# Two moves in GpSimd's queue of a two-layer decoder trunk: where heads 2 and 5 are staged

## The chip, the core and the metric

One core of a Trainium2 chip runs the whole program. The time is the device time of one execution in microseconds (us); lower is better. Engines are named as the profile names them: PE is TensorE (PEld its weight loads), DVE is VectorE, ACT is ScalarE, POOL is GpSimd, SP is SyncE, which issues transfers. Each engine works through its own queue in order and meets the others at semaphores only.

## What is computed

Two layers (`DEPTH = 2`) over one sequence of 512 rows of width 1024, all in float32. Cut to what matters here:

```
for l in range(2):
    h    = rms_norm(x) * (1 + sc) + sh
    proj = h @ w_in[l]
    y_ssd  = Mamba-2 scan: 4 chunks of 128 rows, 8 heads of 64, SiLU gate, grouped RMS norm
    y_mla  = 4 heads, q and k of width 96 from low-rank (latent) projections with rotary part,
             RMS norm of q and k per head, dense causal attention
    y_moba = 4 heads, q and k of width 64 straight from proj, RMS norm per head,
             causal attention with a bias by distance
    x = x + g * (concat(norm(y_ssd), norm(y_mla), norm(y_moba)) @ w_out[l])
    x = x + g' * mixture_of_experts(...)      # 16 experts, top 2
```

## The kernel before, in words

A hardware loop runs the same program for both layers. In a layer the stages follow one another: the input projection, the mixers (this case), the output projection, the router and the experts. The mixer stage is written as one order by hand for each engine.

**Heads.** The eight attention heads are taken in the order `HEADS = [6, 7, 4, 5, 0, 1, 2, 3]`: the number h that the code passes around (0 to 7) is the place in this list. Places 0 to 3 are the four MoBA heads, places 4 to 7 the four MLA heads. "The third head" is h = 2, a MoBA head; "the sixth" is h = 5, the second MLA head. For each head:

- `stage(h)` on GpSimd (from L2417) multiplies the head's rows of q and k by their reciprocal norms and writes them to a pair of row buffers, `staged(h)`: two instructions for a MoBA head (both recorded at L2415), three for an MLA head. MoBA heads use `moba_rows[h % 2]` in slot 2 of `ring`, MLA heads use `mla_rows[h % 2]` in `work`. For h in 2, 3, 6, 7 it first waits until the head two places before it has been turned (`qk_ps`). It ends by counting up `stg`.
- `turn_q(h)` and `turn_k(h)` on TensorE (L1042, L1054) wait for `stg` and transpose the rows; VectorE (`q_out`, L2030) and ScalarE (`k_out`, L1515) take them out.
- `scores(n)` on TensorE (L1069), n = 4 h + t for the row tiles t = 0 to 3; `biased(n)` on VectorE (L2045) adds the bias and takes the maximum; `expo(n)` on ScalarE (L1527); `turn_p(n)` (L1084) and `pv(n)` (L1100) on TensorE; `head_out(h)` on VectorE (L2050, L2051).

**Chunks.** The first four heads run beside the four chunks c = 0 to 3 of the scan, head c beside chunk c. A chunk has `xs_rows` (L960), `decay` (L975, L978), `bm_rows` (L966, L968), `y_off` (L986), `state` (L998) and `y_diag` (L1012) on TensorE, and `chunk_dt` (L1947, L1949), `decay_difference` (L1957), `chunk_scores` (L1967), `chunk_y` (L1986, L1987) and others on VectorE. `turn_q(c + 1)` stands right behind `y_off(c)` in TensorE's queue. `y_diag(c)` counts up `yd_ps`; `chunk_y(c)` counts up `y_dn`. The buffers of a chunk are doubled (`xs`, `xdt`, `xde`, index c % 2): `xs` is `work[s0 : s0 + 1024]`, `xdt` is `work[s0 + 1024 : s0 + 2048]`. `skip(c)` (L2409) on GpSimd makes the product of `xs` with the skip weights for chunk c.

**Latent projections.** Beside chunk 0 TensorE makes the MLA q and k/v rows (`mla_qkv(0)` to `(3)`, L1028, L1031), ScalarE copies them out and counts up `qkv_ev` to 8 (L1505, L1507). Then GpSimd turns the rotary parts (`rope(0)` to `rope(4)`, six instructions each, L2449 to L2456, done: `kr_dn`), VectorE sums the squares (`mla_squares`, L2007 and L1923, done: `hss`), and GpSimd takes the power -1/2 (`rstd`, L2369, L2370).

**Late modulation.** Between its other work VectorE adds up the modulation of the next half (`late_adds`, L1735, L1739, three additions to two tiles), from chunk 2 on.

**Behind the chunks** come the tiles n = 16 to 31 of the MLA heads. For n = 16 TensorE's queue begins with `turn_q(5)`, `turn_k(5)`, `scores(18)`, `turn_p(16)`, `pv(15)`.

**GpSimd's queue** in this stage, before (each `wait` blocks all that stands behind it):

```
stage(0)  store_ada_rows(1)  skip(0)  stage(1)
wait qkv_ev 8   rope(0) rope(1) skip(1) rope(2) rope(3) rope(4)
stage(2)  skip(2)   wait hss 2   rstd   stage(3)  skip(3)  stage(4)
wait y_dn 4   stage(5)   wait ysq 8   rstd   y_norm ...  stage(6)  y_norm ...  stage(7)
```

Of the kernel before, what the change touches and what calls it, by code (L numbers as in the profile page):

```python
# [112 lines left out]
def trunk(nc, A, out, cpack, bucket_oh, relv, hf_rows, y_rows, mod_rows):  # L113
# [10 lines left out]
    def sem(name):  # L124
        sems.append(ctx.enter_context(nc.semaphore(name)))
        return sems[-1]
# [28 lines left out]
    def view(off, *dims, of=work):  # L155
        n = int(np.prod(dims))
        v = of[:, off:off + n]
        if len(dims) == 2:
            return v.rearrange("p (a b) -> p a b", a=dims[0])
        if len(dims) == 3:  # L160
            return v.rearrange("p (a b c) -> p a b c", a=dims[0], b=dims[1])
        return v
# [5 lines left out]
    s0 = 10944  # L168
# [13 lines left out]
    p_cols = [actT[:, 6:8, :], view(16384, 2, 512)]  # L182
    y_scratch = view(s0 + 768, 256)
    moba_rows = [[ring[:, 2, 2816 + 512 * n + 256 * m:3072 + 512 * n + 256 * m] for m in range(2)] for n in range(2)]
    mla_rows = [[view(18624 + 384 * m, 384) for m in range(2)], [view(s0 + 384 * m, 384) for m in range(2)]]
    rtmp = ring[:, 2, 0:1280].rearrange("p (a b) -> p a b", a=4)
    sq = ring[:, 2, 1280:2816]
    sq_moba = view(17408, 1024)
# [60 lines left out]
    def hi_chunk(j, k):  # L249

        _, a0, _, buf = next(h for h in hi_parts if h[0] == j and h[1] <= k < h[2])
        return buf[:, 512 * (k - a0):512 * (k - a0) + 512]
# [122 lines left out]
    yd_ps = sem("y_diag_in_psum")  # L375
# [298 lines left out]
    def staged(h):  # L674
        q, k = moba_rows[h % 2] if h < 4 else mla_rows[h % 2]
        return tuple(a.rearrange("p (t n) -> p t n", t=T) for a in (q, k))
# [15 lines left out]
    with nc.Fori(0, DEPTH) as L:  # L692
# [3 lines left out]
        with nc.Block() as block:  # L696
# [154 lines left out]
            def _(pe):  # L851
# [55 lines left out]
                for i, b in enumerate(IN_ORDER):  # L907
                    wd = in_width[b]
                    w_parts = [in_part(b, half) for half in range(2)]
                    for t in range(T):  # L910
                        n = group_no[("in", b, t)]
                        bank_free(n)
                        if i == 0:
                            pe.wait_ge(hl_dn, 2 * t + 2)
                        for k in range(KD):
                            if i and t == 0 and k % 4 == 0:
                                pe.wait_ge(in_w_lo, 2 * i + k // 4 - 1)
                            if i == 0 and k == 4 and t < T - 1:
                                to_columns(t + 1)
                            _, lo, hi = (ap.rearrange("p (k n) -> p k n", k=4)[:, k % 4, :] for ap in w_parts[k // 4])  # L920
                            hh, hl = actT_r[:, k, :], hL[:, k, :]
                            for m, (w_, h_) in enumerate(((hi, hl), (lo, hh), (hi, hh))):
                                first_, last_ = k == 0 and m == 0, k == KD - 1 and m == 2
                                if b in (1, 2):
                                    mm = pe.matmul(ps[n % 2][:, :], w_[:, P * t:P * t + P], h_, start=first_, stop=last_)
                                else:
                                    mm = pe.matmul(ps[n % 2][:, 0:wd], h_[:, P * t:P * t + P], w_, start=first_, stop=last_)  # L927
                        mm.then_inc(acc_ps, 1)
                        if n == T:
                            pe.wait_ge(hl_dn, 2 * T)  # L930
                            pe.wait_ge(par, 14 * 16)
                            pe.transpose(ps[2][:, 0:64], prow[:], cst[0:64, C_ID:C_ID + 64]).then_inc(pcol_ps, 1)
                        if n in ADA_AFTER:
                            ada_total(ADA_AFTER[n], ps[6 + ADA_AFTER[n] % 2])
# [255 lines left out]
                def out_products(b, t, ks, opens=False, closes=False):  # L1190
                    n = group_no[("out", b, t)]
                    for k in ks:
                        if t == 0 and k % 4 in (0, 2):
                            pe.wait_ge(out_w_lo, 2 * b + k // 4 + 1)
                        _, lo, hi = (ap.rearrange("p (k n) -> p k n", k=4)[:, k % 4, :] for ap in out_part(b, k // 4))
                        yh, yl = (ap[:, k, P * t:P * t + P] for ap in (actT_r, yL))
                        pe.matmul(ps[n % 2][:, :], yl, hi, start=opens and k == ks[0], stop=False)
                        pe.matmul(ps[n % 2][:, :], yh, lo, start=False, stop=False)
                        mm = pe.matmul(ps[n % 2][:, :], yh, hi, start=False, stop=closes and k == ks[-1])
                    if closes:  # L1200
                        mm.then_inc(acc_ps, 1)
# [1162 lines left out]
            def _(g):  # L2364
# [37 lines left out]
                def skip(c):  # L2402
                    g.wait_ge(xs_cp, c + 1)
                    if c > 0:
                        g.wait_ge(y_dn, c)
                    else:
                        g.wait_ge(h_ps, 2 * T)
                        g.wait_ge(par, 14 * 16)
                    g.tensor_tensor(xd.rearrange("p (h n) -> p h n", h=NH), xs[:, c % 2, :].rearrange("p (h n) -> p h n", h=NH),  # L2409
                                    hpar[:, 2, :].unsqueeze(2).to_broadcast([P, NH, HP]), ALU.mult).then_inc(xd_dn, 1)  # L2410
# [3 lines left out]
                def times_rstd(dst, src, rstd_, n):  # L2414
                    return g.tensor_tensor(dst, src, rstd_.to_broadcast([P, T, n]), ALU.mult)  # L2415

                def stage(h):  # L2417

                    if h in (2, 3, 6, 7):
                        g.wait_ge(qk_ps, 2 * h - 2)  # L2420
                    q3, k3 = staged(h)
                    hd = HEADS[h]
                    hh = hd % MH
                    c0 = 0 if hd < MH else 32
                    rq = rs_h[:, c0:c0 + 16].rearrange("p (t h) -> p t h", t=T)[:, :, hh:hh + 1]
                    rk_ = rs_h[:, c0 + 16:c0 + 32].rearrange("p (t h) -> p t h", t=T)[:, :, hh:hh + 1]
                    if hd < MH:
                        if hd == 0:
                            g.wait_ge(hrs, 2)
                        step(times_rstd(q3, qrow[:, :, DQ * hh:DQ * hh + DQ], rq, DQ))  # L2430
                        step(times_rstd(k3[:, :, 0:DN], kv[:, :, 128 * hh:128 * hh + DN], rk_, DN))
                        times_rstd(k3[:, :, DN:DQ], kr, rk_, DR).then_inc(stg, 1)
                    else:
                        step(times_rstd(q3[:, :, 0:HP], proj[:, :, MQ0 + HP * hh:MQ0 + HP * hh + HP], rq, HP))
                        times_rstd(k3[:, :, 0:HP], proj[:, :, MK0 + HP * hh:MK0 + HP * hh + HP], rk_, HP).then_inc(stg, 1)
                    g.wait_ge(stg, h + 1)
# [8 lines left out]
                def rope(h):  # L2445
                    src = qrow[:, :, DQ * h + DN:DQ * h + DQ] if h < MH else proj[:, :, KR0:KR0 + DR]
                    x1, x2 = src[:, :, 0:16], src[:, :, 16:32]
                    ta, tb, tc, td = (rtmp[:, k, 64 * h:64 * h + 64].rearrange("p (t n) -> p t n", t=T) for k in range(4))
                    g.tensor_tensor(ta, x1, cos, ALU.mult).then_inc(gch, 1)  # L2449
                    g.tensor_tensor(tb, x2, sin, ALU.mult).then_inc(gch, 1)  # L2450
                    g.tensor_tensor(tc, x1, sin, ALU.mult).then_inc(gch, 1)
                    g.tensor_tensor(td, x2, cos, ALU.mult).then_inc(gch, 1)
                    step.n += 4
                    g.wait_ge(gch, step.n)
                    step(g.tensor_tensor(x1, ta, tb, ALU.subtract))
                    ins = g.tensor_tensor(x2, tc, td, ALU.add)  # L2456
                    if h < MH:
                        step(ins)
                    else:
                        ins.then_inc(kr_dn, 1)  # L2460
# [4 lines left out]
                store_ada_rows(1)  # L2465
                skip(0)
                stage(1)
                g.wait_ge(qkv_ev, 2 * T)
                rope(0)
                rope(1)  # L2470
# [1 line left out]
                rope(2)  # L2472
                rope(3)
                rope(4)
                stage(2)
                skip(2)
                g.wait_ge(hss, 2)
                rstd(rs_h[:, 0:32], ss_h[:, 0:32], DQ, hrs)
                stage(3)
                skip(3)  # L2480
                stage(4)
                g.wait_ge(y_dn, T)
                stage(5)
                g.wait_ge(ysq, 8)
                rstd(rs_y[:, 0:8], ss_y[:, 0:8], 256, yrs)
                g.wait_ge(yrs, 1)
# [110 lines left out]
```

## Time and profile before

| what | value |
|---|---|
| median of 3 runs | 1477.59 us (1475.14 to 1477.91) |
| span of the profiled execution | 1470.7 us |
| PE busy | 1323.4 us, 90% |
| DVE busy | 1162.9 us, 79% |
| ACT busy | 739.2 us, 50% |
| POOL busy | 239.1 us, 16% |
| DMA | 382.29 MB, mean 260 GB/s |
| mixer stage, layer 0 | about 190 to 333 us of the span |
| mixer stage, layer 1 | about 901 to 1040 us of the span |

The span is from the first to the last instruction of one execution. A row of the timeline gives the start, the time busy, the engine, the line, the operation and its operands, how many instructions were merged, and in brackets how long the engine stood idle before it and who released it. A releaser is inferred from semaphore events.

### The profile page before, as it was taken

To read this page: it belongs to the slowest core of one execution; us is meant where nothing else is said; L and a number is where in the kernel's file an instruction comes from. 1 tells how busy PE (TensorE), PEld (TensorE's weight loads), DVE (VectorE), ACT (ScalarE), POOL (GpSimd) and SP (SyncE) were. 2 spreads that over 40 slices of the span, in tenths; PEclk is the share of its full clock that TensorE was granted. 3 is DMA by queue.
4 is the path that set the end of the run, shared out by engine and by line. 5 is a ranking of instruction groups with operands and counts; after the bars stand their busy time and mean duration, and the time that the engine had idled before them with its cause. 6 is when DMAs were issued, how large, how long until landed. Compare 5 with 4: busy or idle time off the path is not lost. (4 is left out here: it accounts for less than half of the span.)

```text
span 1470.7 us, 17413 instructions
## 1 busy us (share of the span) xinstructions
PE 1323.4 (90%) x6467; PEld 1048.2 (71%) x6467; DVE 1162.9 (79%) x1379; ACT 739.2 (50%) x969; POOL 239.1 (16%) x296
## 2 busy tenths in 40 slices
PE   6799987889989999999949998878998999999993
PEld 2577865667878888888747777566777788888871
DVE  3569856885579999999855988488656999999986
ACT  1334333562437777777413343447223877777750
POOL 0100125431011000000121012345110100000002
PEclk9899988989999999999979999898999999999996
DMA  9676621433579999999558483133347999999965
GB/s 357 240 261 223 203 90 59 143 100 131 218 283 361 413 411 416 407 402 376 196 180 294 170 270 120 58 115 115 130 152 287 362 404 407 413 404 407 403 225 197
DMA packets 96788, 382.29 MB, mean 260 GB/s; under 512 B 6009, under 2 KB 8807, under 8 KB 86968
## 3 DMA queue, kind: packets, MB, share of 16 engines
q1 hardware_dynamic: 73144, 311.50, 55.9%
q0 software_dynamic: 15232, 55.63, 9.7%
q10 hardware_dynamic: 8320, 13.96, 2.7%
q8 instruction: 55, 0.90, 0.2%
q14 instruction: 37, 0.30, 0.1%
HBM read 348.25 MB, written 32.82 MB: 259 GB/s over the span
## 5 line engine op out<-in xcount | busy, mean ns | idle before, releaser
L1274 PE MATMUL ps<-mod_rounded,work_rounded 128*128 128x512 f32 x340 | 136.9, 403 | 1.1 <-DVE work_rounded L2281 1.1
L1276 PE MATMUL ps<-mod_rounded,work_rounded 128*128 128x512 f32 x340 | 134.4, 395 | 0.0
L1275 PE MATMUL ps<-ring_rounded,work_rounded 128*128 128x512 f32 x288 | 113.7, 395 | 0.0
L1735 DVE SCALAR_TENSOR_TENSOR gain<-ring,csil,gain 128x512 f32<-128x512 f32 x134 | 104.3, 778 | 3.3
L2140 DVE TENSOR_TENSOR ring_rounded<-ring,mod_rounded 128x2048 fp32r<-128x2048 f32 (+1 forms) x54 | 102.8, 1929 | 1.4
L1275 PE MATMUL ps<-work_rounded 128*128 128x512 f32 x256 | 101.0, 395 | 0.0
L2140 DVE TENSOR_TENSOR work_rounded<-work,mod_rounded 128x2048 fp32r<-128x2048 f32 (+1 forms) x48 | 91.3, 1930 | 9.6 <-ACT mod_rounded L1635 8.4
L927 PE MATMUL ps<-ring_rounded,actT_rounded 128*128 128x512 f32 (+1 forms) x256 | 93.4, 365 | 0.0
L2512 POOL DMA_INDIRECT work<-ffn_rows,slot_idx x34 | 42.0, 1234 | 302.9 <-PE ps L1260 270.1
L1635 ACT ACTIVATE mod_rounded<-ring 128x2048 fp32r<-128x2048 f32 (+1 forms) x54 | 85.9, 1625 | 0.0
L1276 PE MATMUL ps<-actT_rounded,work_rounded 128*128 128x512 f32 x204 | 80.4, 394 | 0.0
L1655 ACT ACTIVATE work_rounded<-ps 128x512 fp32r<-128x512 f32 x68 | 37.2, 596 | 85.7 <-PE ps L1260 85.7
L927 PE MATMUL ps<-work_rounded,mod_rounded 128*128 128x512 f32 (+1 forms) x192 | 76.6, 399 | 4.0 <-ACT work L1402 4.0
L1274 PE MATMUL ps<-actT_rounded,work_rounded 128*128 128x512 f32 x204 | 80.1, 393 | 0.0
L1635 ACT ACTIVATE mod_rounded<-work 128x2048 fp32r<-128x2048 f32 (+1 forms) x48 | 76.4, 1624 | 0.0
L1274 PEld LDWEIGHTS ps<-mod_rounded,work_rounded 128*128 128x128 f32 x340 | 64.0, 188 | 15.1 <-DVE work_rounded L2281 1.6
L1276 PEld LDWEIGHTS ps<-mod_rounded,work_rounded 128*128 128x128 f32 x340 | 63.9, 188 | 14.7
L901 PE MATMUL ps<-cst 128*128 128x128 f32 x360 | 51.2, 303 | 24.2 <-issue 14.6
L927 PE MATMUL ps<-work_rounded,actT_rounded 128*128 128x512 f32 (+1 forms) x192 | 72.5, 377 | 0.0
L2140 DVE TENSOR_TENSOR ring_rounded<-ring,actT_rounded 128x3072 fp32r<-128x3072 f32 x18 | 60.4, 3356 | 12.2 <-ACT actT_rounded L1635 12.2
L901 PEld LDWEIGHTS ps<-cst 128*128 128x128 f32 x360 | 48.1, 216 | 26.8 <-issue 26.7
L2527 POOL DMA_DIRECT2D expert_rows<-work x32 | 18.1, 566 | 298.3 <-DVE work L2275 298.3
(370 smaller groups left out, 3635.9 us busy)
## 6 DMA issues: line engine op xcount, KB each, us to landing
ring<-in_ada_w SPq DMA_DIRECT2D x38, 1024.0 KB, 5.2
ring<-in_moe_w_gate SPq DMA_DIRECT2D x18, 2048.0 KB, 10.1
ring<-in_moe_w_up SPq DMA_DIRECT2D x18, 2048.0 KB, 10.4
ring<-in_moe_w_down SPq DMA_DIRECT2D x18, 2048.0 KB
work<-in_moe_w_up SPq DMA_DIRECT2D x16, 2048.0 KB, 10.6
work<-in_moe_w_down SPq DMA_DIRECT2D x16, 2048.0 KB, 11.6
work<-in_moe_w_gate SPq DMA_DIRECT2D x16, 2048.0 KB, 10.3
expert_rows<-work POOLq DMA_DIRECT2D x32, 512.0 KB, 7.7
```

Source lines behind the costliest of these rows:

```text
L901: pe.matmul(ps[7][:, 0:P], ident, ident, start=True, stop=True)
L927: mm = pe.matmul(ps[n % 2][:, 0:wd], h_[:, P * t:P * t + P], w_, start=first_, stop=last_)
L1274: pe.matmul(ps[j][:, :], xl, hi, start=k == 0, stop=False)
L1275: pe.matmul(ps[j][:, :], xh, lo, start=False, stop=False)
L1276: mm = pe.matmul(ps[j][:, :], xh, hi, start=False, stop=k == KD - 1)
L1635: a.activation(buf, slots[3 * odd + j][:, 512 * k0:512 * k1], ACT.Copy).then_inc(w_hi, 1)
L1655: a.activation(xeT_r[:, 4 * j:4 * j + 4, :], ps[2 + j][:, :].rearrange("p (k n) -> p k n", k=4), ACT.Copy).then_inc(xt_ev, 1)
L1735: add(v.scalar_tensor_tensor(acc, w, csil[:, k:k + 1], acc, ALU.mult, ALU.add))
L2140: v.tensor_tensor(slots_r[3 * odd + j][:, 512 * k0:512 * k1], slots[3 * odd + j][:, 512 * k0:512 * k1], buf.bitcast(F32), ALU.subtract).th ...
L2512: g.indirect_dma_start(out=dst, out_offset=None, in_=hf_rows, in_offset=bass.IndirectOffsetOnAxis(ap=col, axis=0)).then_inc(sem_, 16)
L2527: g.dma_start(yv[e - 4], ysb[:, e % 2, :]).then_inc(yw[e % 2], 16)
```

## The change

Three edits. `stage(2)` moves in GpSimd's queue from behind `rope(4)` to directly behind `stage(1)`, which is ahead of the wait for `qkv_ev`. `stage(5)` moves from behind the wait `y_dn >= 4` to ahead of it, and gets a wait of its own, `yd_ps >= 3`. And the second row buffer pair of the MLA heads, used by h = 5 and 7, moves its k rows from `work[s0 + 384 : s0 + 768]` to `work[s0 + 1024 : s0 + 1408]`: before, they lay across both `xs` buffers, of which the second belongs to chunk 3; after, q lies on `xs[0]` and k on `xdt[0]`, which belong to chunk 2, the third.

```diff
-    mla_rows = [[view(18624 + 384 * m, 384) for m in range(2)], [view(s0 + 384 * m, 384) for m in range(2)]]
+    mla_rows = [[view(18624 + 384 * m, 384) for m in range(2)], [view(s0 + 1024 * m, 384) for m in range(2)]]
...
                 skip(0)
                 stage(1)
+                stage(2)
                 g.wait_ge(qkv_ev, 2 * T)
...
                 rope(4)
-                stage(2)
                 skip(2)
...
                 stage(4)
+                g.wait_ge(yd_ps, 3)
+                stage(5)
                 g.wait_ge(y_dn, T)
-                stage(5)
                 g.wait_ge(ysq, 8)
```

## Rows read from the trace of the kernel before

**Rows 1.** The page: span, and busy time of an engine, share, instructions

```profile
span 1470.7 us, 17413 instructions
...
PE 1323.4 (90%) x6467; PEld 1048.2 (71%) x6467; DVE 1162.9 (79%) x1379; ACT 739.2 (50%) x969; POOL 239.1 (16%) x296
```

**Rows 2.** Waits of PE, 186 to 349: us in total, times, longest

```profile
PE ps L1042 <- POOL ring L2415: 5.2, 1, 5.2
...
PE ps L1042 <- POOL work L2415: 2.7, 1, 2.7
```

**Rows 3.** Timeline of GpSimd, layer 0

```profile
197.08 1.66 POOL L2415 TENSOR_TENSOR ring<-work,sml 128x256 f32<-128x256 f32 x2
...
222.88 1.30 POOL L2449 TENSOR_TENSOR ring<-actT,cst 128x64 f32<-128x64 f32 x1 [24.14 <-ACT mod L1507]
...
236.20 1.32 POOL L2415 TENSOR_TENSOR ring<-work,sml 128x256 f32<-128x256 f32 x2
...
257.72 1.67 POOL L2415 TENSOR_TENSOR ring<-work,sml 128x256 f32<-128x256 f32 x2
...
271.88 0.91 POOL L2415 TENSOR_TENSOR work<-work,sml 128x128 f32<-128x128 f32 x1
283.15 1.21 POOL L2415 TENSOR_TENSOR work<-actT,sml 128x384 f32<-128x384 f32 x1 [10.37 <-DVE work L1987]
...
285.47 0.41 POOL L2415 TENSOR_TENSOR work<-work,sml 128x128 f32<-128x128 f32 x1
```

**Rows 4.** Timeline of PE, layer 0, and the last row from layer 1

```profile
197.74 0.63 PE L1054 MATMUL ps<-cst,ring 128*64 128x128 f32 x4 [1.78 <-DVE mod L2030]
...
231.26 1.08 PE L986 MATMUL ps<-work 128*128 128x256 f32 x4
237.57 1.06 PE L1042 MATMUL ps<-cst,ring 128*64 128x128 f32 x4 [5.23 <-POOL ring L2415]
...
263.51 1.90 PE L1012 MATMUL ps<-work 128*128 128x64 f32 x16
...
282.35 0.87 PE L1069 MATMUL ps<-mod 96*128 96x128 f32 x4
285.93 0.64 PE L1042 MATMUL ps<-cst,work 128*96 128x128 f32 x4 [2.70 <-POOL work L2415]
...
944.14 1.06 PE L1042 MATMUL ps<-cst,ring 128*64 128x128 f32 x4 [5.24 <-POOL ring L2415]
```

**Rows 5.** Stretches: length, busy us (x) by engine, granted clock, DMA share, GB/s

```profile
199.67:231.26 31.59, 28.72 (x126) 17.76 (x126) 12.12 (x28) 13.10 (x34) 7.91 (x17) 0.84 0.30 102
910.64:937.82 27.18, 24.32 (x126) 16.00 (x126) 12.10 (x28) 13.14 (x34) 7.91 (x17) 1.00 0.37 127
231.26:246.96 15.70, 10.47 (x54) 7.63 (x53) 5.47 (x10) 2.86 (x7) 5.55 (x17) 0.67 0.00 1
...
258.87:266.30 7.43, 7.43 (x53) 6.11 (x53) 6.63 (x14) 2.97 (x7) 0.51 (x1) 1.00 0.12 31
...
291.81:298.43 6.62, 6.62 (x23) 5.12 (x24) 5.52 (x8) 5.29 (x18) 6.19 (x6) 0.51 0.25 66
```

**Rows 6.** Timeline of VectorE, layer 0

```profile
247.50 1.75 DVE L1923 TENSOR_TENSOR ring<-actT 128x1536 f32<-128x1536 f32 x1
...
284.95 0.29 DVE L2045 CUSTOM_DVE_ANT_0 mod<-ps,cst 128x128 f32<-128x128 f32 x1
...
286.61 0.75 DVE L2030 TENSOR_SCALAR mod<-ps,pcol 96x512 f32<-96x512 f32 x1 [1.36 <-PE ps L1042]
...
299.07 0.75 DVE L2030 TENSOR_SCALAR mod<-ps,pcol 96x512 f32<-96x512 f32 x1 [1.64 <-PE ps L1042]
```

**Rows 7.** L1967 (190 to 285), L1735 (282 to 284.9): min/median/max ns, starts

```profile
L1967 DVE TENSOR_TENSOR work<-work x8: 672/681/1073, 198.2 to 278.2; 128x512 f32<-128x512 f32 x8
...
L1735 DVE SCALAR_TENSOR_TENSOR gain<-ring,csil,gain x2: 744/974/1205, 282.9 to 283.7; 128x512 f32<-128x512 f32 x2
```

## The prediction

> **What bounds the kernel now.** I read the page first. The span is 1470.7 us and TensorE is busy for 90% of it, GpSimd for 16% [rows 1]. So a change that only moves GpSimd's work can gain just where TensorE stands still for GpSimd, and the question is how much it stands, where, and what is late next. The waits of TensorE in one mixer stage answer the first part: it waits for the staging line twice, 5.2 us once (MoBA rows, `ring`) and 2.7 us once (MLA rows, `work`) [rows 2]. The timeline of TensorE puts them: 5.23 us ahead of `turn_q(2)` at 237.57, and 2.70 us ahead of `turn_q(5)` at 285.93; layer 1 repeats the first with 5.24 us at 944.14 [rows 4]. GpSimd's timeline shows the other side: it idles 24.14 us until 222.88, when the latent projections have been copied out, then does the ropes up to 236.20, and `stage(2)` stands behind them and takes 1.32 us; later it idles 10.37 us until 283.15 and then does `stage(5)`, which ends at 285.47 + 0.41 = 285.88 [rows 3]. TensorE starts 0.05 us after that. Both waits are on the path: before 237.57 and before 285.93 VectorE and ScalarE have nothing left either that TensorE's next result doesn't release.
>
> Third, the windows, for the clock. The stretch from `y_off(1)` to the next chunk's first scores, 231.26 to 246.96, takes 15.70 us at a mean granted clock of 0.67; the same sequence one chunk later, 258.87 to 266.30, takes 7.43 us at 1.00 [rows 5]. So the 5.23 us are not all: the wait is followed by work at TensorE's lower level of 1.2 GHz instead of 2.4 (four transposes in 1.06 us at 237.57, against 0.63 at 197.74 [rows 4]).
>
> **Edit A, `stage(2)` ahead of the latent wait.** It removes two instructions from behind the ropes and adds them behind `stage(1)`. Its own wait, that `turn_k(0)` has been done, ends at 197.74 + 0.63 = 198.37 [rows 4]; `stage(1)` ends at 197.08 + 1.66 = 198.74 [rows 3]. So `stage(2)` runs from 198.74 to about 200.1 and GpSimd is back at its wait 22 us before that ends: the ropes, `skip(1)` and the rest are not delayed. Nothing else is in the queue that it passes (no transfer is issued between the two places).
> - Gain: `turn_q(2)` follows `y_off(1)` directly, as `turn_q(3)` follows `y_off(2)`. Chunk 1 then looks like chunk 2: 15.70 - 7.43 = **8.27 us**, of which 5.23 is the wait and 3.04 the work at the lower clock. The chunk that I compare with has even more VectorE work in it (x14 against x10 [rows 5]), so it is no flattering model.
> - What is late next? `mla_squares(1)` on VectorE needs the ropes. It starts at 247.50 [rows 6] and would start at 239.2; the ropes end at 236.20. The cover is 3.0 us. The ropes still to be done at 232 now run beside VectorE work instead of beside nothing; if they stretch by more than 3 us, the surplus is lost. After that `stage(3)` waits for these squares, so it moves with them: it ends at 257.72 + 1.67 = 259.39 [rows 3], and `turn_q(3)` comes behind `y_off(2)`, which starts at 258.87 and needs about 1 us; the margin of half a us is kept because both sides hang on the same `chunk_y(1)`.
> - Cost: the new place is busy on VectorE. `chunk_scores(0)` has two instructions of L1967. The median of the eight in the four chunks is 0.68, the longest takes 1.07 [rows 7]; asked for alone it is the first, at 198.2, beside `stage(1)` [rows 3]. The second, up to 199.9, will run beside `stage(2)` and `y_diag(0)` waits for it. I take the row's own stretch, 1.07 - 0.68 = 0.39 us; the bounds are 0 and 2 x 0.39. A gain is excluded: nothing there waits for GpSimd.
>
> The Trainium skill's page "SBUF - State Buffer", section "Who interferes with whom", speaks against this edit: VectorE with two SBUF inputs and GpSimd take a shared port pair in turn, and the later one blocks for the whole instruction of the other. By that rule L1967 would wait for what is left of the first instruction of `stage(2)`, some 0.2 us as an estimate, and edit A would stand 0.2 us better. In the row here GpSimd's side stretched too (1.66 us for `stage(1)` against 1.32 for `stage(2)`), so the trace does not fit a lock with one loser, and the rows decide.
>
> Edit A: 8.27 - 0.39 = **7.88 us a layer**.
>
> **Edit B, `stage(5)` ahead of `y_dn`, on other buffers.** The buffer edit costs nothing in itself: same shapes, same instructions. The new wait, `yd_ps >= 3`, is met when `y_diag(2)` is done, 263.51 + 1.90 = 265.41 [rows 4], while `stage(4)` ends at 271.88 + 0.91 = 272.79 [rows 3]. So it costs nothing, and nothing queued behind it (the `y_dn` wait, `rstd`, the eight `y_norm`s, `stage(6)`) is held: all of it waited beyond 283 before. `stage(5)` runs from 272.8 to about 275.5.
> - Gain: TensorE's 2.70 us are not given back whole, since VectorE is next. TensorE is done with its scores at 282.35 + 0.87 = 283.22 [rows 4] and turns q of head 5 by 283.9. VectorE must first finish two late additions and `biased(16)` at 284.95 [rows 6]. The additions take 744 and 1205 ns, the second beside `stage(5)` [rows 7]; without it they take 2 x 0.74, so `biased(16)` starts 0.46 earlier, at 284.49, and ends at 284.78. Then `q_out(5)` follows at once, where it stood at 286.61 [rows 6]: 286.61 - 284.78 = **1.83 us**.
> - Cost: in its new place `stage(5)` meets `chunk_scores(3, 0)`, L1967 again, at 272.9, and the following `decay_difference` carries a stretch on to ScalarE and TensorE. 0 to 0.46 us (the stretches seen); I take 0.39.
>
> Edit B: 1.83 - 0.39 = **1.44 us a layer**. If the first additions of n = 16 are not relieved it is 1.0, and 2.7 is the most that the wait holds.
>
> **Sum.** 7.88 + 1.44 = 9.32 us a layer, 18.6 for two. The loads of the mixer and of the experts are issued on counts that move with the work, and those issued at a fixed time are used over 20 us later, so I expect no stage behind to give any of it back. The profiled execution has 1470.7 us of span; 1470.7 - 18.6 = 1452.1. The median of the runs lies 1477.6 - 1470.7 = 6.9 us above the span. That gives **1459.0 us**, -1.26%.
>
> **Rivals.**
> 1. *The clock falls once or twice more, or once in another place.* The chain of chunk 0 shows the price: 31.59 us at 0.84 in layer 0 and 27.18 at 1.00 in layer 1, for the same instructions [rows 5], 4.41 us. Everything in layer 1 will sit about 10 us earlier, and the fall of layer 0 may appear there too: 1463.4; with a second one 1467.8. The Trainium skill, page "TensorE: Matmul & The Clock Gate", section "What's actually happening", says that the point at which the clock rises varies between runs of the same kernel. By that the falls may land anew after any shift. The trace agrees so far as the two layers differ in chunk 0. Against it: the later stretches cost the same in both layers.
> 2. *The clock gives back more.* From 291.81 to 298.43 TensorE works at 0.51, and VectorE idles 1.64 us for it at 299.07 [rows 5, 6]. If the fuller stretch around 284 keeps the clock up, that wait goes in both layers: 3.3 us more, 1455.7; with the cost terms at their lower bounds 1454.1, and if layer 0's fall in chunk 0 went too (nothing ahead of it changes), about 1450.
> 3. *Only the wait goes.* The clock stays at the lower level through chunk 1: 5.23 instead of 8.27, 6.1 us less in all, 1465.1. Rows against it: the clock fell only in the gap itself (the stretches before have 0.84 and 1.00, and TensorE was packed up to 231).
> 4. *The wait moves.* `turn_q(2)` or what follows finds something equally late, so the change doesn't do what it says: 1475 to 1478. For it: the queue is dense with waits. Against it: `q_sb`, `k_sb` and `stg` are all that `turn_q(2)` asks for, and the first two are met before 221.
> 5. *Slower.* One mechanism: with the packing changed, TensorE drops to its lower level in the chunks and stays there. Each such fall costs 4.41 us; it decides from the fifth on (18.6 / 4.41 = 4.2), which gives 1481 and more. The stage has three of them a layer now. Port stretches can't do it alone: ten VectorE instructions at 0.46 each are 4.6 us a layer, half the gain.
>
> **How the numbers follow.** Forecast 0.47 (its own range, from the bounds of the costs and one small shift of the clock, 1455.5 to 1462.5), rival 1 0.23, rival 2 0.17, rival 3 0.06, rival 4 0.04, rival 5 0.03. Taking in rivals 1 and 3 up to two falls and rival 2 but for its far end, the range is 1451 to 1468. It leaves out some 0.12. A measurement of this kernel tells about 0.2% (3 us) from no change. All cases but 4 and 5 lie below 1474.6: faster 0.93, the same 0.04, slower 0.03.
>
> **What would show it.** Right for A: `turn_q(2)` starts within 0.2 us of the end of `y_off(1)`, no wait of TensorE on the `ring` rows, the stretch from `y_off(1)` to the next chunk's scores takes 7.4 to 8 us at a clock near 1.00, and L2415 appears at 198.7. Right for B: `stage(5)` at 272.8 less the shift, no wait on it, `q_out(5)` right behind `biased(16)`. Wrong: `y_diag(0)` later by over 0.8 us, the ropes ending after `chunk_y(1)`, or the mixer stage of layer 1 not being shorter by about the same as that of layer 0. If the stretches outside the mixer stages change their lengths by over a us, my claim that nothing behind gives anything back is wrong.

## The result

The changed kernel took 1467.4 us in the median of five runs (1457.55 to 1468.42), against 1477.59; the ratio is 0.9932, 95% interval 0.9908 to 0.9956. Run again beside the experiments it took 1461.5 (six runs, 1452.01 to 1470.34; ratio 0.9892, 0.9863 to 0.9922). The kernel before took 1475.7 us in the mean of the 57 runs made beside the experiments (1475.8 with the five made beside the first result) and the changed one 1462.9 in the mean of all its 11. The change is worth **12.8 us, 0.9%**. The forecast was 18.6 us. The sign held, and so did the range (1451 to 1468), but by 0.6 us for the first median of 1467.4, which is luck; the size did not.

The profiled execution of the changed kernel is its fastest of the first five: a span of 1455.9 us, 1457.55 with what lies around it. That is 1.65 us around the span, so 5 of the 6.9 us that the prediction set between the span and the median of the kernel before were no overhead: its profiled execution was a fast one too. (Over its 57 runs the time lies 1.6 to 2.9 us above the span.)

Of the page of the changed kernel, against [rows 1]:

```profile
span 1455.9 us, 17415 instructions
...
PE 1319.3 (91%) x6467; PEld 1045.3 (72%) x6467; DVE 1162.8 (80%) x1379; ACT 738.9 (51%) x969; POOL 246.8 (17%) x296
```

GpSimd does the same 296 instructions, but is busy 7.7 us longer: some of them now run beside VectorE and stretch.

The waits of TensorE in layer 0, 186 to 349 (us in total, times, longest), against [rows 2]:

```profile
PE ps L1084 <- ACT mod L1527: 6.8, 8, 2.1
PE ps L1069 <- DVE sml L2045: 6.5, 7, 1.8
PE ps L1165 <- DVE work_rounded L2105: 1.9, 2, 1.3
```

Both waits for the staging line L2415, 7.9 us, are gone. The waits for L1527 and L2045 grew by 2.1 us together (5.4 to 6.8 and 5.8 to 6.5); no single new wait took the place of the two. The timelines of GpSimd and of TensorE, against [rows 3, 4]:

```profile
200.29 3.99 POOL L2415 TENSOR_TENSOR ring<-work,sml 128x256 f32<-128x256 f32 x4
221.70 1.30 POOL L2449 TENSOR_TENSOR ring<-actT,cst 128x64 f32<-128x64 f32 x1 [17.42 <-ACT mod L1507]
...
236.72 0.32 POOL L2456 TENSOR_TENSOR work<-ring 128x64 f32<-128x64 f32 x1
...
266.14 0.83 POOL L2415 TENSOR_TENSOR work<-actT,sml 128x384 f32<-128x384 f32 x1
```

```profile
230.07 1.08 PE L986 MATMUL ps<-work 128*128 128x256 f32 x4
230.99 0.60 PE L1042 MATMUL ps<-cst,ring 128*64 128x128 f32 x4
...
250.19 1.06 PE L1042 MATMUL ps<-cst,ring 128*64 128x128 f32 x4
```

`stage(2)` is the second half of the row at 200.29 and GpSimd is back at the latent wait 17 us ahead of its end; `stage(5)` begins at 266.14 directly behind `stage(4)`. `turn_q(2)` starts at 230.99, in the tail of `y_off(1)`, in 0.60 us instead of 1.06. But `turn_q(3)` at 250.19 now takes 1.06, where it had taken 0.60. The windows show what that is. Columns as in [rows 5]: length, busy us (x) of PE, PEld, DVE, ACT, POOL, granted clock, DMA share, GB/s; from `y_diag(0)` to `y_off(1)`, to `xs_rows(2)`, to `y_off(2)`, to `xs_rows(3)`, to `y_off(3)`, to the output projection, and in layer 1 from `y_off(2)` to `xs_rows(3)`:

```profile
203.28:230.07 26.79, 23.93 (x124) 15.73 (x124) 11.71 (x27) 13.14 (x34) 8.82 (x19) 1.00 0.35 119
230.07:237.50 7.43, 7.43 (x54) 6.11 (x53) 5.40 (x10) 2.86 (x7) 6.35 (x15) 1.00 0.00 1
237.50:248.90 11.40, 7.50 (x49) 5.56 (x49) 11.09 (x21) 4.71 (x14) 7.36 (x4) 1.00 0.01 1
248.90:259.58 10.68, 10.68 (x53) 7.83 (x53) 6.52 (x13) 2.98 (x7) 0.90 (x2) 0.68 0.11 25
259.58:269.78 10.20, 7.36 (x49) 5.56 (x49) 9.99 (x18) 4.89 (x14) 6.89 (x7) 1.00 0.75 283
269.78:325.48 55.70, 45.99 (x263) 34.66 (x262) 45.55 (x91) 37.04 (x87) 22.02 (x22) 0.88 0.35 116
948.83:957.90 9.07, 9.07 (x53) 6.81 (x53) 6.53 (x13) 2.97 (x7) 0.90 (x2) 0.81 0.14 24
```

The stretch from `y_off(1)` to the next chunk went from 15.70 to 7.43 us, to the hundredth what the prediction said, at a clock of 1.00. The stretch one chunk later, which had served as its model with 7.43 at 1.00 [rows 5], now takes 10.68 us at 0.68 in layer 0 and 9.07 at 0.81 in layer 1.

One stretch of the kernel before, which the prediction did not read, lies between its two. It is `xs_rows(2)` to `y_off(2)`; below it is one row of TensorE's timeline from inside it:

```profile
246.96:258.87 11.91, 9.01 (x49) 6.72 (x49) 11.22 (x20) 4.77 (x14) 7.77 (x5) 0.86 0.00 1
254.57 1.92 PE L978 MATMUL ps<-cst,sml 128*128 128x128 f32 x8
```

So the kernel before had a second fall, in chunk 2, in both layers (`decay` in 1.92 us where it takes 1.05 at the full clock). It lay where TensorE waits anyway and was over before `y_off(2)`: the stretch takes 11.91 us against 11.40 in the changed kernel, at 1.00. After the change TensorE goes through that stretch at the full clock here and falls just behind it, within work without a gap. The low clock behind the first wait is gone; the fall of chunk 2 comes later and costs 3.25 and 1.64 us where it had cost 0.5.

By these profiles the mixer stages, from L946 to the output projection, went from 143.53 to 132.69 us and from 139.13 to 130.97. That is 19.0 us, but 4.4 of it is the fall in chunk 0 of layer 0 [rows 5], which no edit touches and which is absent in this execution. Outside the mixer stages it lost 4.2 us: 189.58 to 192.79 ahead of the first, 567.44 to 567.26 between them, 431.02 to 432.19 behind. The stretches ahead of the first stage and behind the second took 189.27 and 431.17 us in another profiled execution of the same changed kernel, so these differences are spread between executions and no effect of the edits.

### The profile page after: what moved, and what is told of

Read it like the earlier page. It is cut to its first block and busy times, and to the rows that moved or that the text cites. A ratio compares the mean times of both kernels' runs of the same rounds, so it can differ in the third digit from the quotient of the medians.

```text
span 1455.9 us, 17415 instructions
## 1 busy us (share of the span) xinstructions
PE 1319.3 (91%) x6467; PEld 1045.3 (72%) x6467; DVE 1162.8 (80%) x1379; ACT 738.9 (51%) x969; POOL 246.8 (17%) x296
## 5 line engine op out<-in xcount | busy, mean ns | idle before, releaser
L1735 DVE SCALAR_TENSOR_TENSOR gain<-ring,csil,gain 128x512 f32<-128x512 f32 x134 | 102.4, 764 | 3.3
## 6 DMA issues: line engine op xcount, KB each, us to landing
ring<-in_moe_w_gate SPq DMA_DIRECT2D x18, 2048.0 KB, 10.5
work<-in_moe_w_up SPq DMA_DIRECT2D x16, 2048.0 KB, 11.1
```

Source lines behind the costliest of these rows:

```text
L1735: add(v.scalar_tensor_tensor(acc, w, csil[:, k:k + 1], acc, ALU.mult, ALU.add))
```

## The experiments

Two theories were tested. **Theory 1**: both the wait and the slow work behind it (5.23 and 3.04 us a layer) leave with edit A. **Theory 2**: only the waits leave; the time at the lower clock moves on. "The stretch from `y_off(1)`" and the like are read from the windows as above.

### Each edit alone

```diff
# a_alone: the kernel before, with
                 stage(1)
+                stage(2)
                 g.wait_ge(qkv_ev, 2 * T)
...
                 rope(4)
-                stage(2)
# b_alone: the changed kernel, with these two lines put back as they were before
```

> The kernel before with stage(2) moved ahead of the latent wait, and nothing else. Theory 1 (the forecast's own sum: 8.27 us a layer from y_off(1) to the next chunk, less up to 0.39): 15 to 16.5 us less than the kernel before, and what the changed kernel's runs lack is in edit B or in the clock at other places. Theory 2 (the wait goes, but TensorE falls to its lower clock a chunk later, as in layer 0 of the changed kernel's trace): 8 to 11 us less, runs spread over more than 5 us, and in the profile 3 to 4 us more from y_off(2) to the next chunk than the 7.43 us of before. In the profile y_off(1) to the next chunk takes 7.4 us by both.

> The changed kernel with stage(2) put back behind the ropes: edit B and its buffers alone. Theory 1 (the sum: 1.44 us a layer): 2 to 4 us less than the kernel before. Theory 2 (the new place stretches chunk_scores(3, 0) by the 0.66 us that the changed kernel's trace shows, so half of it is given back): 0 to 3 us less. The wait of 2.70 us on the work rows is gone by both, and VectorE's q_out(5) comes about 1.8 us earlier relative to biased(16).

Measured, `a_alone`: 1466.6 us in the median of 12 runs beside 1475.4 (ratio 0.9939, 0.9912 to 0.9966), 8.8 us less, the runs from 1461.1 to 1476.1. That is theory 2's size: twice the wait is 10.5, with the clock's share it would be 16.5. Its windows, chunk 1 and the two stretches behind it in layer 0, then chunk 1 of layer 1:

```profile
229.70:237.13 7.43, 7.43 (x53) 6.11 (x53) 5.39 (x10) 2.85 (x7) 6.34 (x15) 1.00 0.00 1
237.13:249.40 12.27, 9.69 (x49) 7.08 (x49) 11.54 (x21) 4.84 (x15) 8.14 (x5) 0.77 0.00 1
249.40:260.65 11.25, 11.25 (x52) 8.29 (x53) 6.41 (x13) 2.89 (x7) 0.16 (x1) 0.65 0.11 19
936.49:945.56 9.07, 9.07 (x54) 6.91 (x53) 5.60 (x10) 2.85 (x7) 5.63 (x15) 0.81 0.01 2
```

In layer 0 chunk 1 is at 7.43 and chunk 2 pays 3.82 of that back (11.25 against 7.43); in layer 1 a fall lies in chunk 1 itself, and the stretch behind chunk 2 pays 1.52 (8.95). My statement that the first stretch takes 7.4 us by both theories was wrong for layer 1.

`b_alone`: 1474.6 in the median of 12 beside 1475.4 (ratio 0.9999, 0.9967 to 1.0031): nothing that the runs can tell. The profile resolves it. The stretch from `xs_rows(3)` to `y_off(3)`, and from there to the output projection:

```profile
266.99:277.19 10.20, 7.36 (x50) 5.56 (x49) 9.99 (x18) 4.89 (x14) 6.89 (x7) 1.00 0.75 282
277.19:332.76 55.57, 44.51 (x263) 34.13 (x262) 45.81 (x91) 36.98 (x87) 22.34 (x22) 0.91 0.35 117
```

Before, these two took 9.55 and 57.26. So edit B takes 1.69 us off behind and puts 0.65 on ahead, 1.0 a layer, 2.1 us in all. (Of the 1.69 a little may be clock, 0.91 against 0.88; the changed kernel, at 0.88 like the kernel before, has 55.70 and 55.62, which is 1.6 us off.) The interval of the ratio, 4.6 us to either side, contains that and zero.

### Where the 0.65 us are

```diff
                 g.wait_ge(yd_ps, 3)
+                g.wait_ge(seg_dn, 2 * T)
                 stage(5)
```

`seg_dn` is counted up by `decay_difference`, so `stage(5)` now starts behind it.

> The changed kernel with one more wait ahead of stage(5), for decay_difference(3, 1): it then no longer runs beside chunk_scores(3, 0), which it stretches from 0.68 to 1.34 us in the changed kernel's trace. If that stretch is on the path, the stretch from the fourth chunk's xs_rows to y_off(3) goes back from 10.20 to 9.55 us and the time falls by 1.3 us in all, which the runs' spread may hide; if not, the stretch is the same and only the rows differ.

In the changed kernel's timeline of VectorE `chunk_scores(3, 0)` runs beside the first instruction of `stage(5)`, and takes 1.34 us where the median of L1967 is 0.69:

```profile
266.19 1.34 DVE L1967 TENSOR_TENSOR work<-work 128x512 f32<-128x512 f32 x1
267.45 0.68 DVE L1957 TENSOR_TENSOR work<-ps,sml 128x512 f32<-128x512 f32 x1
```

With the later start the stretch is back at its old length:

```profile
260.83:270.37 9.54, 7.35 (x49) 5.55 (x49) 9.33 (x17) 4.88 (x14) 5.55 (x6) 1.00 0.81 306
```

That holds in both layers. The time, 1458.7 us in the mean of 6 runs (median 1459.8) against 1462.9 for the changed kernel, goes the right way by more than the 1.3 us that this explains, but the six runs spread over 18 us, so it shows nothing by itself. The profile does: the stretch was contention, and it was on the path.

### Filling the wait instead of removing it

```diff
                 def turn_q(h):
-                    pe.wait_ge(stg, h + 1)
                     if h > 0:
                         pe.wait_ge(q_sb, h)
                         pe.wait_ge(k_sb, h)
+                    if h == 2:
+                        for _ in range(40):      # before_fill20: 20
+                            pe.matmul(ps[0][:, 0:P], ident, ident, start=True, stop=True)
+                    pe.wait_ge(stg, h + 1)
```

> The kernel before; TensorE makes 40 identity products of 128x128 into the free bank of turn_q(2) while it waits for stage(2), so the wait stays and TensorE is not idle in it. The products add no result. Theory 1 (3.04 of the 8.27 us are the lower clock behind the wait, and it falls because TensorE is idle): about 3 us a layer less, 6 in all, granted clock near 1.00 from y_off(1) to the next chunk, which takes about 12.7 us. Theory 2 (the clock is worth less over the whole, since it falls elsewhere instead): 0 to 3 us less and a fall in chunk 2 or 3 that the kernel before doesn't have.

> The kernel before with 20 identity products in TensorE's wait ahead of turn_q(2) instead of 40: 40 took 9.1 us where the wait has 5.2, since each is two instructions; 20 should take 4.6 and so lie inside the wait. The products add no result. Theory 1 (holding the clock up through the gap is worth 3.04 us a layer): 5 to 7 us less than the kernel before, mean clock 0.959. Theory 2 (the fall comes later instead): 0 to 3 us less, mean clock 0.955 or less, in the profile the stretch from y_off(1) to the next chunk at 12.5 us but a fall in chunk 2 that the kernel before doesn't have.

`before_fill` took 1484.5 us, 9 more than the kernel before, and is a mis-sized experiment: a product of two float32 operands is recorded as two instructions here, so 40 took 9.10 us in a gap of 5.2. `before_fill20` is the right one; its timeline of TensorE:

```profile
226.87 1.08 PE L986 MATMUL ps<-work 128*128 128x256 f32 x4
227.79 4.63 PE L1040 MATMUL ps<-cst 128*128 128x128 f32 x40
233.19 0.62 PE L1045 MATMUL ps<-cst,ring 128*64 128x128 f32 x4 [0.78 <-POOL ring L2418]
```

and its windows, from `y_off(1)` on:

```profile
226.87:239.73 12.86, 12.08 (x94) 10.66 (x93) 5.38 (x10) 2.86 (x7) 5.56 (x17) 1.00 0.01 2
239.73:251.99 12.26, 9.69 (x49) 7.06 (x49) 11.54 (x21) 4.84 (x15) 8.11 (x5) 0.77 0.00 0
251.99:263.23 11.24, 11.24 (x53) 8.30 (x53) 6.42 (x13) 2.90 (x7) 0.16 (x1) 0.65 0.07 24
```

Holding the clock up through the gap took the stretch from 15.70 to 12.86 us, so the 2.84 us of slow work behind the wait are real. And they were given back: `xs_rows(2)` to `y_off(2)` went from 11.91 to 12.26 and the next stretch from 7.43 to 11.24 (9.44 in layer 1). The expectation calls a fall in chunk 2 one that the kernel before doesn't have; it had one (0.86, above), but one that was over before the work without a gap. The time was 1473.9 in the median of 12 beside 1475.1, ratio 0.9994 (0.9969 to 1.002), so a gain of over 4.6 us lies outside the interval, and with it theory 1's 5 to 7. This kernel has every wait of the kernel before and none of the moves: the share of the clock alone brought no gain that the runs can tell.

### Holding the clock up behind it

TensorE has more waits of 0.9 to 2.1 us, for VectorE and ScalarE, that no edit touches. In chunk 2 they cluster, beside VectorE's sums of squares (4.4 us from 238.04 on in the changed kernel). They can be filled with products into a free bank:

```diff
+                def warm(count):
+                    for _ in range(count):
+                        pe.matmul(ps[0][:, 0:P], ident, ident, start=True, stop=True)
...
                         mla_qkv(0)
+                    warm(6 if c == 2 else 0)     # late_warm5, before_warm5, after_fill_c2: 3
                     scores(n + 1)
+                    warm(6 if c == 2 else 0)     # 3
                     turn_p(n)
...
                     scores(n + 2)
+                    warm(10 if c > 0 else 0)     # 5; after_fill_c2: 5 if c == 2
                     turn_p(n + 1)
...
+                        if n in (18, 22):        # not in after_fill_c2
+                            pe.wait_ge(q_sb, n // T + 2)
+                            warm(10)             # 5
                         scores(n + 2)
```

> The changed kernel; TensorE makes 6 to 10 identity products of 128x128 in the waits of 0.9 to 2.1 us that are left in chunks 1 to 3 and ahead of scores(20) and scores(24). They add no result. Theory 1 (what the changed kernel's median of 1467.4 lacks to the forecast of 1459 is TensorE at its lower clock in the mixer stages): 1455 to 1461 in the median, runs within 4 us of one another, no fall of the clock in chunks 1 to 3. Theory 2 (it is lost elsewhere, before the mixers or in the experts): the same as the changed kernel or up to 3 us more for the products.

> The changed kernel with identity products (3, 3 and 5) in the three short waits of TensorE in chunk 2 alone, the stretch in which VectorE sums the squares of the MLA rows. They add no result. If it is this thin stretch that makes the clock fall behind it, the stretch from y_off(2) to the next chunk goes from 9.1 to 11.2 us back to 7.4 to 7.6 in both layers and the time is 3 to 7 us below the changed kernel's mean of 1462.9; if the fall has another cause, it stays at 9 us and more.

> The changed kernel with the later stage(5) and with half as many identity products in TensorE's short waits as before (3 to 5 instead of 6 to 10; those took 12.58 us from xs_rows(2) to y_off(2) where the changed kernel takes 11.40). The products add no result. If a small number holds the clock up: 1450 to 1456 in the median at a mean clock of 0.965 to 0.97. If the number matters: mean clock below 0.962 and 1458 or more.

`after_warm`: 1456.1 in the median of 6 (1453.2 to 1462.7), mean clock 0.968, and no fall in chunks 1 to 3 of its profile. That is theory 1's time, but the runs spread over 9 us, not 4, and the 6 to 10 products were too many: chunk 2 took 12.58 us for 11.40. `after_fill_c2`, three smaller fills in one chunk: 1456.7 (1451.2 to 1462.6), mean clock 0.961. Its chunk 2 and the stretch that had fallen:

```profile
236.73:248.14 11.41, 10.35 (x72) 8.17 (x71) 11.10 (x21) 4.71 (x14) 7.37 (x4) 1.00 0.01 1
248.14:255.70 7.56, 7.56 (x54) 6.03 (x53) 6.43 (x13) 2.97 (x7) 0.89 (x2) 1.00 0.13 32
```

The products cost nothing in chunk 2 (11.41 against 11.40 for the same work), and the stretch behind is at 7.56 in both layers. So the fall behind chunk 2 comes from the thin TensorE work in it. But part of the fall moved on once more: `xs_rows(3)` to `y_off(3)` takes 10.55 and 10.47 us where it took 10.20, and from there to the output projection it is 56.84 and 56.86 where it was 55.70 and 55.62. The two mixer stages take 131.05 and 130.99 us, which is no more than 1.6 below those of the profiled execution of the changed kernel. The gain of its runs, 6.0 us between the means, is sized by few runs. `late_warm5`: 1455.5 (1452.9 to 1459.1) at 0.963; in time the small number does as much as the large one, and its mean clock lies between the two forecasts.

All traced layers together, as length in us and granted clock, layer 0 and layer 1 (the last two kernels are told of below):

```
kernel               xs_rows(2) to y_off(2)     y_off(2) to xs_rows(3)
before               11.91 0.86   11.91 0.86     7.43 1.00    7.43 1.00
b_alone              11.91 0.86   11.91 0.86     7.43 1.00    7.43 1.00
changed              11.40 1.00   11.40 1.00    10.68 0.68    9.07 0.81
changed, once more   12.27 0.76   11.41 1.00    11.15 0.65   10.68 0.68
after_late           12.27 0.76   12.26 0.76    11.19 0.65   11.18 0.65
a_alone              12.27 0.77   11.77 0.85    11.25 0.65    8.95 0.82
before_fill20        12.26 0.77   12.27 0.75    11.24 0.65    9.44 0.78
before_fill          12.27 0.76   11.76 0.83    11.18 0.65    8.79 0.84
after_fill_c2        11.41 1.00   11.41 1.00     7.56 1.00    7.57 1.00
after_warm           12.58 1.00   12.58 1.00     7.43 1.00    7.43 1.00
late_warm5           11.41 1.00   11.41 1.00     7.57 1.00    7.57 1.00
before_warm5         11.41 1.00   11.41 1.00     7.62 1.00    7.62 1.00
late_warm_all        11.40 1.00   11.40 1.00     7.56 1.00    7.56 1.00
```

Where the wait ahead of `turn_q(2)` is left bare, the packed stretch is at the full clock in all four layers. Where it is removed or filled and chunk 2 is left thin, the stretch takes 8.8 to 11.3 us in all twelve. Where chunk 2 is filled too, it is back at 7.4 to 7.6.

### The moves with the clock held in both

> The kernel before with identity products in all of TensorE's longer waits of the mixer stage: 20 ahead of turn_q(2), 8 ahead of turn_q(5), 3 to 5 in the short waits of chunks 1 to 3 and ahead of scores(20) and scores(24). The products add no result. With the clock held up in both, this kernel and late_warm5 (1455.6 mean) differ by the two waits alone. Theory 2 (the moves are worth their waits, 5.23 and about 1.7 us a layer, the clock is a separate matter): 1468 to 1471, mean clock 0.963 or more, no stretch from y_off(2) to the next chunk over 8 us. Theory 1 (the moves also keep the clock up): this kernel stays above 1472, since its waits are still there.

`before_warm5` is the kernel before with the same fills as `late_warm5` and 20 and 8 products ahead of `turn_q(2)` and `turn_q(5)`. (`late_warm5` also has the later `stage(5)`, so the 0.65 us of contention are not in it.) It took 1467.7 in the median of 6 runs, 1468.5 in the mean, at a mean clock of 0.9645; `late_warm5` took 1455.6 in the mean at 0.9632. No stretch from `y_off(2)` to the next chunk is over 8 us in either. With the clock held up in both, the two moves are worth 12.9 us between these means; 11.1 if each is first set against the runs of the kernel before beside it (8.1 and 19.2 us less). The waits alone make 2 x (5.23 + 1.69) = 13.8. In the profiles `y_off(1)` to `xs_rows(2)` is 12.85 against 7.43 us, and `y_off(3)` to the output projection 56.40 against 54.73 in layer 0. Theory 2 had put this kernel at 1468 to 1471, theory 1 above 1472.

### The fall in chunk 0, and a faster kernel

```diff
                 decay(0, 1)
+                warm(6, 1)      # into ps[1]; the second argument is the bank
                 turn_k(0)
...
                     else:
+                        warm(6, 3)
                         mla_qkv(0)
```

> late_warm5 with 6 more identity products ahead of turn_k(0) and 6 ahead of mla_qkv(0), in chunk 0, where the stretch from y_diag(0) to y_off(1) takes 26.8 us at the full clock and 29.4 to 31.4 where it fell. They add no result. If the waits of 1.6 to 1.8 us there make the clock fall: 26.8 to 27.5 us in both layers, mean clock 0.966, 1450 to 1454 in the median. If not, the same as late_warm5, 1455.5.

`late_warm_all` took **1446.8 us** in the median of 5 runs (1445.1 to 1447.8) beside 1476.2, ratio 0.9795 (0.9773 to 0.9817): better than my expectation, 29 us below the kernel before and 16 below the changed one. From `y_diag(0)` to `y_off(1)` in layers 0 and 1, and below them the same stretch of layer 1 in `late_warm5`, where the clock had fallen:

```profile
200.27:227.07 26.80, 26.57 (x147) 18.27 (x146) 11.72 (x27) 13.13 (x34) 8.85 (x19) 1.00 0.37 122
897.64:924.43 26.79, 26.56 (x146) 18.25 (x146) 11.71 (x27) 13.13 (x34) 8.83 (x19) 1.00 0.35 119
```

```profile
900.24:931.62 31.38, 29.75 (x134) 18.69 (x134) 11.73 (x27) 13.08 (x34) 8.83 (x19) 0.84 0.28 91
```

It is also the only kernel here whose runs agree within 3 us. The two stretches of chunk 0 explain at most 4.6 us of the 8.9 that it lies under `late_warm5`. Of the 7.8 us between the two profiled spans, 4.7 lie outside the mixer stages, where nothing was changed (191.39 to 189.80 ahead of the first, 570.42 to 567.29 between them). Where the rest of the mean comes from I did not trace run by run.

### What the spread is

The changed kernel was run once more, to size the clock's share over more runs than five:

> The changed kernel once more, for its own spread and beside the others of this call. Over its five runs the mean granted clock was 0.953, over 29 runs of the kernel before 0.953 too, and in either kernel a run with 0.01 less clock takes about 10 us more. Theory 2 (the wait of TensorE goes, the time at the lower clock doesn't, it lies elsewhere): 9 to 12 us less than the kernel before at the same mean clock. Theory 1 (the lower clock goes too): mean clock of 0.958 or more, 16 to 19 us less.

Measured: 1461.5 us in the median of six runs (1452.0 to 1470.3, mean clock 0.957), ratio 0.9892 (0.9863 to 0.9922), between what the two theories say. Its profiled execution took 1470.3 at 0.948, the slowest of the six, and the stretch from `y_off(2)` to `xs_rows(3)` had fallen there too:

```profile
248.81:259.96 11.15, 11.15 (x53) 8.30 (x53) 6.40 (x13) 2.89 (x7) 0.15 (x1) 0.65 0.11 17
```

These two profiled executions of one program stand 12.8 us apart, as much as the whole change is worth in the mean. A single profiled execution can't size it.

Each run comes with its mean granted clock:

```
kernel          runs   mean us   mean clock (lowest to highest)
before            57    1475.7   0.953 (0.941 to 0.958)
a_alone           12    1467.0   0.955 (0.950 to 0.959)
b_alone           12    1475.7   0.953 (0.941 to 0.961)
before_fill       12    1483.7   0.955 (0.946 to 0.964)
before_fill20     12    1474.9   0.956 (0.946 to 0.966)
changed           11    1462.9   0.955 (0.948 to 0.965)
after_late         6    1458.7   0.958 (0.951 to 0.963)
before_warm5       6    1468.5   0.965 (0.961 to 0.967)
after_warm         6    1456.9   0.968 (0.963 to 0.971)
after_fill_c2      6    1456.9   0.961 (0.954 to 0.967)
late_warm5         5    1455.6   0.963 (0.961 to 0.965)
late_warm_all      5    1446.7   0.969 (0.968 to 0.970)
```

Within one kernel, a run with 0.01 less clock takes about 11 us more (a line through each kernel's runs, with one slope for all). The fall that the kernel before has behind `turn_q(2)` lowers its mean: 15.70 us at 0.67 in each layer is 2 x 15.70 x 0.33 / 1471 = 0.007. Had it just gone, the changed kernel would stand at 0.960, where its two runs at 0.960 and 0.961 took 1457.0 and 1457.6, near the forecast of 1459.0. Its mean is 0.955.

## Why the prediction was right or wrong, point by point

- **The bound, and the place of the waits**: right. Both waits of TensorE on L2415 are gone, and `turn_q(2)` starts in the tail of `y_off(1)` in both layers.
- **Edit A, the wait (5.23 us a layer)**: right. `a_alone` gained 8.8 us in the median, and twice the wait is 10.5, within its interval (5 to 13 us).
- **Edit A, the slow work behind it (3.04 us a layer)**: this is the term that failed. The step was "Chunk 1 then looks like chunk 2", which is true (7.43), together with "I expect no stage behind to give any of it back", which is not: chunk 2 no longer looks like chunk 2. The model stretch was at the full clock right behind a fall in its own chunk (0.86), which the prediction had not read. `before_fill20` tried the term alone and found no gain, 4.6 us at most. Twice 3.04 is 6.1 us, and the forecast missed by 5.8 (18.6 against 12.8); the two smaller errors below (0.39 a layer too much cost in A, 0.4 too much gain in B) cancel.
- **Edit A, contention with L1967 (0.39)**: too high. From L946, the start of the mixer stage, to `y_diag(0)` it is 10.48 us for 10.47, and from `y_diag(0)` to `y_off(1)` 26.79 for 26.80 at the same clock. VectorE's second L1967 was not stretched; GpSimd's instruction was (1.55 us for 0.62). The Trainium skill, page "SBUF - State Buffer", section "Who interferes with whom", has the shared ports as an exclusive lock, and the order of issue decides who waits. The trace agrees in part: the staging instruction started at 202.03, behind the first L1967 (201.43 to 202.49), and stretched; but it also started ahead of the second (202.42), which did not. Beside `stage(5)` it agrees plainly: L1967 started 0.04 us behind GpSimd's instruction and took 1.34 us.
- **Ropes as cover for `mla_squares(1)`**: right. They end at 236.72 + 0.32 = 237.04 and stretched by about 2 us; the squares start at 238.04. The cover of 3.0 us shrank to 1.0.
- **Edit B, the gain (1.83)**: 1.69 measured, right. **Its cost (0.39, bound 0.46)**: 0.65 measured, outside my bound, since L1967 met the longer instruction of an MLA head. Net 1.0 a layer for 1.44.
- **Around the span**: 1.65 us, not 6.9; a wrong reading of the three runs, with no effect on the difference.
- **The two signs of being wrong**: both came up. The mixer stage of layer 1 got 8.2 us shorter and that of layer 0 10.8; without the fall in chunk 0 of layer 0 it would be 6.4 against 8.2, by the larger fall behind chunk 2. And the stretches outside changed by 3.2 and 1.2 us. The changes outside are the spread between executions told of above, but what was said not to be given back was given back inside the stage.
- **Rivals**: rival 3 (only the wait goes, 1465.1, given 0.06) had the size, but its mechanism, a clock that stays low in chunk 1, was wrong; that the size fits is luck. Rival 1 (one or two more falls, 1463.4 and 1467.8, given 0.23) had the mechanism: a fall in another place. It was wrong to treat such a fall as a mishap of the shift. It was the regular consequence (all twelve layers of the table above), and belonged in the likeliest case. That the two layers of the one trace repeated one another to 0.1 us behind chunk 0 misled me: over the runs the falls move.
- The kernel can still lose or gain 5 us between runs of the same program. Which event decides, in a given run, whether a thin stretch makes the clock fall is not settled.

## What to carry to other kernels

A wait that ends in slow TensorE work has two prices: the wait itself, which goes when it is removed, and the clock behind it, which goes only if nothing thin follows. Before counting the second, read the granted clock and TensorE's busy share in every stretch behind, also in the one that lies just ahead of the stretch you take as your model. Here the fall came behind 7.5 us of work in 11.4. A few products without use in the thin stretches (3 to 5 in a wait of 0.9 to 2.1 us) cost nothing there and kept the clock up, but one filled stretch alone handed part of the fall on to the next. With all of them filled, the two moves and the later `stage(5)` it was 29 us, with the moves alone 12.8.

## What the runs showed of the hardware that I had not expected

- One program's runs on one core differ by up to 19 us (1469.0 to 1487.8 in 29 runs of the kernel before on one chip), and the mean granted clock goes with it (0.957 in the fastest, 0.941 in the slowest). One profiled execution shows one placing of the falls.
- Between a GpSimd and a VectorE instruction, both with two SBUF inputs, either can be the one that stretches: L1967 from 0.68 to 1.34 us beside `stage(5)`, the staging instruction from 0.62 to 1.55 beside the two L1967 in chunk 0.
